# The first two modulation vectors as products on TensorE, and a group of small vectors moved to ScalarE's queue

## The chip, the cores and the metric

The kernel runs on one core of one Trainium2 chip. The metric is the device time of one execution in microseconds (us); lower is better.

## The reference

Two transformer blocks run one after the other over a sequence of 1024 tokens with 1024 channels, all in 32-bit floats. Block one is a gated short-convolution layer and a stick-breaking attention layer; block two has sliding-window and differential attention and a convolutional feed-forward layer. Each layer's input is normalised and modulated, and this is what the change touches:

```python
def modulation(c, w, b, n):
    m = jax.nn.silu(c) @ w + b          # c: 1 x 1024, w: 1024 x 3072
    return jnp.split(m, n, axis=-1)

def modulated_norm(x, g, shift, scale):
    return rmsnorm(x, g) * (1.0 + scale[:, None, :]) + shift[:, None, :]

shift, scale, gate = modulation(c, mod_w, mod_b, 3)   # first layer
h = modulated_norm(x, norm_g, shift, scale)
proj = h @ w_in
```

There are fourteen modulation vectors of 1024 numbers in all, each a product of a vector of 1024 with a matrix of 1024 x 1024. The first two, shift and scale of the first layer, are needed before the first large product `h @ w_in` can begin.

## The kernel before, in words

The activations stand transposed: `X[:, j, t]` holds channel `128*j + partition` of token `t`, in KC = 8 tiles of 128 channels and two halves of 512 tokens. Every large product splits both operands in two parts (`w_hi`, `w_lo` and `opA` or `opB` with parts 0 and 1) and takes three matmuls for each tile; these units, L1255, and pairs of units, L1287, are nearly all the work of TensorE. The program is written out by hand, engine by engine, with semaphores; each engine runs its instructions in the order of its block, and a wait holds back all that stands behind it.

The change lies in the opening, before the first pair of units. There the order is this.

- SyncE's queue loads the small vectors of group 0 into `vec_rows` (L970), rows 0 and 1 of the first modulation matrix into `first_mods[0]` (L978), the eight blocks of `x` into `x_rows` (L984), the rest of the first matrix, the ten small transfers of group 1 and 2 (L970, L990, L992), the first weights, and then the second matrix, `first_mods[1]`. Each matrix comes in eight pieces (`kc`) of 512 KB.
- TensorE transposes group 0 (L1322), then `x` in 16 groups of four (L1333). `norm_sum` (L1303) adds up the squares over the channels; `mod_sum` (L1315) adds a vector that lies spread over 128 partitions.
- ScalarE takes the silu of `c` (L1543), copies each transposed group into `X` (L1550) and squares it (L1529).
- VectorE adds the squares (`sq_add`, L1779) and accumulates the modulation vectors: `first_steps` multiplies each piece of the matrix by its 128 numbers of `c`, one for each partition, and adds them to `mod_acc` (L1860 and L1865). After the eighth piece, `mod_sum` on TensorE adds over the partitions with eight matmuls, each with 128 columns of `mod_acc` as the stationary operand and one column of ones as the moving one. `mod_out` (L1757) adds the bias.
- `parts("a", ...)` on VectorE (L1828, L1836) and `act_parts` on ScalarE (L1507, L1511) then make the operand `opA` tile by tile, and the first pair of units on TensorE (L1287) waits for each tile of it.

The later twelve modulation vectors are accumulated on VectorE between other work, and aren't changed.

Of the kernel before, what the change touches and what calls it, by code (L numbers as in the profile page):

```python
# [12 lines left out]
ALU = mybir.AluOpType  # L13
# [174 lines left out]
def program(nc, a, out, known):  # L188
# [3 lines left out]
    with ctx:  # L192
# [107 lines left out]
        def now(s):  # L300

            return total.get(id(s), 0)
# [660 lines left out]
        def _(sp):  # L963
# [23 lines left out]
            sp.wait_ge(dve_done, at("vec_zero"))  # L987
            vectors(1, ROWS1)
            vectors(2, ROWS2)
            sp.dma_start(small[:, SINK:SINK + 8], a["swa_sinks_2"].to_broadcast([P, 8])).then_inc(vec_in[1], 16)  # L990
            step(vec_in[1], "vec_in", 1, by=16)
            sp.dma_start(lam_rows[:, 0:256], a["diff_lambda_2"].rearrange("o f d -> o (f d)").to_broadcast([P, 256])).then_inc(vec_in[1], 16)  # L992
            step(vec_in[1], "vec_in", 1, by=16)
# [254 lines left out]
        def _(pe):  # L1248
# [57 lines left out]
            def mod_sum(g):  # L1306

                if g < FIRST_MODS:
                    pe.wait_ge(dve_done, at("first_step", g, KC - 1))
                else:  # L1310
                    pe.wait_ge(dve_done, at("mod_step", (g + 1) * MOD_PIECES - 1))
                if g:
                    pe.wait_ge(dve_done, at("mod_out", g - 1))
                for j in range(KC):
                    ins = pe.matmul(PS[:, 6, j:j + 1], mod_acc[:, j * P:(j + 1) * P], ones[:, 0:1], start=True, stop=True)  # L1315
                ins.then_inc(pe_done, 1)
                step(pe_done, "mod_sum", g)


            pe.wait_ge(pool_done, at("consts"))  # L1320
# [3 lines left out]

            for j in range(KC):
# [11 lines left out]
            norm_sum("a", 0)  # L1337
            norm_sum("a", 1)
            mod_sum(0)

# [6 lines left out]
            mod_sum(1)  # L1347
# [76 lines left out]
        def _(act):  # L1424
# [115 lines left out]

            act.wait_ge(dve_done, at("cols"))
# [180 lines left out]
        def _(dve):  # L1722
# [29 lines left out]
            def mod_out(g):  # L1752
# [4 lines left out]
                dve.tensor_tensor(mod[:, g, :], PS[:, 6, 0:KC], cols[:, b:b + KC], ALU.add).then_inc(dve_done, 1)  # L1757
# [91 lines left out]
            def first_steps(g, ks):  # L1849

                for kc in ks:
                    src = SILU_C + 8 * MODS[g][2] + kc
                    c = small[:, src:src + 1]
                    if kc == 0:
                        dve.wait_ge(first_mod_in[g][kc], at("first_mod_in", g, kc))
                        dve.wait_ge(act_done, at("silu_c"))
                        if g:
                            dve.wait_ge(pe_done, at("mod_sum", g - 1))
                        dve.wait_ge(dve_done, now(dve_done))
                        dve.tensor_scalar(mod_acc[:], first_mods[g][:, kc, :], c, None, ALU.mult).then_inc(dve_done, 1)  # L1860
                        step(dve_done, "first_step", g, kc)
                    else:
                        dve.wait_ge(first_mod_in[g][kc], at("first_mod_in", g, kc))
                        dve.wait_ge(dve_done, now(dve_done))
                        dve.scalar_tensor_tensor(out=mod_acc[:], in0=first_mods[g][:, kc, :], scalar=c,  # L1865
                                                 in1=mod_acc[:], op0=ALU.mult, op1=ALU.add).then_inc(dve_done, 1)
                        step(dve_done, "first_step", g, kc)

            first_steps(0, range(2))
            for j in range(KC):  # L1870
                sq_add("a", j, 0)
                sq_add("a", j, 1)
                if j >= 2:
                    first_steps(0, range(j, j + 1))
            mod_out(0)
# [3 lines left out]
            step(dve_done)  # L1879

# [9 lines left out]
            first_steps(1, range(KC))  # L1890
# [252 lines left out]
```

## Time and profile before

| what | before |
|---|---|
| time, median of 3 runs | 3103.62 us (3098.84 to 3111.96) |
| span of the profiled execution | 3091.5 us |
| TensorE matmul busy in it | 2909.7 us, 94% |
| VectorE busy | 1508.1 us, 49% |
| ScalarE busy | 945.4 us, 31% |
| mean granted clock of TensorE | 0.968 |

The span runs from the first to the last instruction; the median lies 12.1 us above it. The views give no time of the profiled execution but its span. A time in a row counts from the span's start. PE is TensorE, PEld its loads of stationary operands, DVE VectorE, ACT ScalarE, POOL GpSimd; SPq and ACTq are the queues in which SyncE and ScalarE issue transfers. A 32-bit float matmul leaves two records, so that the eight matmuls of `mod_sum` show as x16; a transpose leaves one.

### The profile page before, as it was taken

To read this page: it belongs to the slowest core of one execution; us is meant where nothing else is said; L and a number is where in the kernel's file an instruction comes from. 1 tells how busy PE (TensorE), PEld (TensorE's weight loads), DVE (VectorE), ACT (ScalarE), POOL (GpSimd) and SP (SyncE) were. 2 spreads that over 40 slices of the span, in tenths; PEclk is the share of its full clock that TensorE was granted. 3 is DMA by queue.
4 is the path that set the end of the run, shared out by engine and by line. 5 is a ranking of instruction groups with operands and counts; after the bars stand their busy time and mean duration, and the time that the engine had idled before them with its cause. 6 is when DMAs were issued, how large, how long until landed. Compare 5 with 4: busy or idle time off the path is not lost.

```text
span 3091.5 us, 35185 instructions
## 1 busy us (share of the span) xinstructions
PE 2909.7 (94%) x13227; PEld 2331.4 (75%) x13227; DVE 1508.1 (49%) x2270; ACT 945.4 (31%) x1871; POOL 943.4 (31%) x703
## 2 busy tenths in 40 slices
PE   3899999799999999999899999898998999999997
PEld 3688878587786666667688888777886888888886
DVE  5666566632205888874520006775526431451444
ACT  4200001413216787852401007653114110110112
POOL 1233323132234444433233344111332333333321
PEclk7999999899999999999999999898999999999999
DMA  5344444363523333331245125112111111111111
GB/s 194 102 141 144 138 130 143 116 204 123 182 84 96 82 82 82 82 96 48 89 143 191 52 58 164 42 42 82 48 48 41 48 48 48 48 48 48 48 47 70
DMA packets 271510, 287.80 MB, mean 93 GB/s; under 512 B 15043, under 2 KB 216172, under 8 KB 269420
## 3 DMA queue, kind: packets, MB, share of 16 engines
q1 hardware_dynamic: 261580, 241.50, 26.0%
q10 hardware_dynamic: 9760, 44.04, 3.6%
q8 instruction: 105, 1.72, 0.2%
q14 instruction: 65, 0.53, 0.1%
HBM read 228.88 MB, written 56.62 MB: 92 GB/s over the span
## 4 chain that ended last, share of the span: by engine, by line
PE 82%; DVE 9%; ACT 4%; DMA 2%; issue 2%; SPq 0%; POOL 0%; DVEq 0%; ACTq 0%; POOLq 0%
PE PS L1255 63%; PE PS L463 3%; PE PS L1287 3%; PE PS L468 2%; PE PS L600 2%; DVE s_sp L808 1%; DMA mod_raw<-in_w_ada 1%; DVE M L1740 1%; PE PS L569 1%; PE PS L560 1%; PE PS L590 1%; DVE M L1779 1%; PE PS L482 1%; PE PS L1315 1%; DVE s_al L820 1%
## 5 line engine op out<-in xcount | busy, mean ns | idle before, releaser
L1255 PE MATMUL PS<-opA,w_hi 128*128 128x512 f32 x4736 | 1475.7, 392 | 27.3 <-POOL w_lo L1128 11.8
L1255 PEld LDWEIGHTS PS<-opA,w_hi 128*128 128x128 f32 x4736 | 894.7, 189 | 217.2 <-issue 17.1
L1255 PE MATMUL PS<-opA,w_lo 128*128 128x512 f32 x2368 | 925.6, 391 | 0.0
L1123 POOL CAST w_hi<-w_raw 128x1024 fp32r<-128x1024 f32 (+1 forms) x193 | 204.1, 1057 | 1447.9 <-PE PS L1255 1384.6
L1128 POOL TENSOR_TENSOR w_lo<-w_raw,w_hi 128x1024 fp32r<-128x1024 f32 (+1 forms) x198 | 479.3, 2421 | 200.3 <-ACT w_hi L1517 184.8
L1255 PEld LDWEIGHTS PS<-opA,w_lo 128*128 128x128 f32 x2368 | 448.0, 189 | 92.7
L1255 PE MATMUL PS<-opB,w_hi 128*128 128x512 f32 x1216 | 377.9, 391 | 4.4 <-DVE opB L1964 3.4
L1255 PEld LDWEIGHTS PS<-opB,w_hi 128*128 128x128 f32 x1216 | 229.0, 188 | 53.3 <-DVE opB L1964 3.8
L1740 DVE SCALAR_TENSOR_TENSOR M<-mod_raw,small,M 128x512 f32<-128x512 f32 x168 | 186.3, 1109 | 147.7 <-DMA mod_raw<-in_w_ada 70.2
L1255 PE MATMUL PS<-opB,w_lo 128*128 128x512 f32 x608 | 237.2, 390 | 0.0
L1975 DVE SCALAR_TENSOR_TENSOR X<-PS,mod,X 128x512 f32<-128x512 f32 x96 | 72.1, 751 | 290.8 <-PE PS L1255 285.1
L463 PE MATMUL PS<-s_sp,tri 128*128 128x512 f32 (+3 forms) x384 | 167.0, 517 | 19.4 <-DVE s_sp L808 15.5
L808 DVE SCALAR_TENSOR_TENSOR s_sp<-PS,s_t 128x128 f32<-128x128 f32 (+1 forms) x192 | 106.1, 552 | 136.2 <-ACT s_t L678 109.1
L1173 POOL TENSOR_TENSOR s_p<-s_p,s_sp 128x512 f32<-128x512 f32 (+3 forms) x128 | 145.5, 1137 | 63.1 <-DVE s_sp L808 63.1
L820 DVE TENSOR_TENSOR s_al<-s_a,s_ah 128x128 fp32r<-128x128 f32 (+1 forms) x192 | 154.1, 802 | 6.6
L1921 DVE TENSOR_SCALAR yt<-M,cols 128x512 f32<-128x512 f32 x44 | 63.9, 1453 | 164.8 <-ACT M L1687 161.8
L1287 PE MATMUL PS<-opA,w_hi 128*128 128x512 f32 x320 | 118.0, 437 | 21.7 <-DVE opA L1836 21.7
L1687 ACT ACTIVATE M<-PS 128x512 f32<-128x512 f32 x44 | 26.4, 599 | 353.5 <-PE PS L1255 350.9
L1529 ACT ACTIVATE M<-X 128x512 f32<-128x512 f32 x80 | 50.6, 633 | 272.0 <-DVE X L1975 270.7
L1255 PEld LDWEIGHTS PS<-opB,w_lo 128*128 128x128 f32 x608 | 114.6, 188 | 23.8
L468 PE MATMUL PS<-s_p,nones 128*128 128x512 f32 (+3 forms) x320 | 122.5, 465 | 0.0
L653 ACT ACTIVATE s_t<-PS 128x128 f32<-128x128 f32 (+1 forms) x192 | 94.6, 493 | 76.7 <-PE PS L454 42.7
(179 smaller groups left out, 3420.7 us busy)
## 6 DMA issues: line engine op xcount, KB each, us to landing
mod_raw<-in_w_ada SPq DMA_DIRECT2D x96, 256.0 KB, 2.9
w_raw<-in_w_up SPq DMA_DIRECT2D x44, 512.0 KB, 3.8
w_raw<-in_w_in SPq DMA_DIRECT2D x34, 512.0 KB, 3.8
w_raw<-in_a_w_in SPq DMA_DIRECT2D x32, 512.0 KB, 4.8
q_dram<-stage ACTq DMA_DIRECT2D x16, 1024.0 KB, 4.0
hin<-q_dram SPq DMA_DIRECT2D x64, 256.0 KB, 5.5
k_dram<-stage ACTq DMA_DIRECT2D x13, 1024.0 KB, 4.8
mod_raw<-in_b_mod_w SPq DMA_DIRECT2D x48, 256.0 KB, 2.8
```

The source lines that it names most:

```text
L463: ins = pe.matmul(scores_of(g, qs), tri[:], s_sp[:, g % 3, qs:], start=False, stop=True, skip_group_check=True)
L468: ins = pe.matmul(scores_of(g, qp), nones[:], s_p[:, (g - 1) % 3, qp:], start=False, stop=True, skip_group_check=True)
L653: act.activation(s_t[:, g % 3, qs:], scores_of(g, qs), ACT.Abs).then_inc(act_done, 1)
L808: dve.scalar_tensor_tensor(out=s_sp[:, e % 3, qs:], in0=scores_of(e, qs), scalar=0.0, in1=s_t[:, e % 3, qs:], op0=ALU.max, op1=ALU.add).th ...
L820: dve.tensor_tensor(s_al[:, e % 3, qs:], s_a[:, e % 3, qs:], s_ah[:, e % 3, qs:].bitcast(F32), ALU.subtract).then_inc(dve_done, 1)
L1123: pool.tensor_copy(hi, raw).then_inc(pool_done, 1)
L1128: pool.tensor_tensor(lo, raw, hi.bitcast(F32), ALU.subtract).then_inc(pool_done, 1)
L1173: pool.tensor_tensor(s_p[:, g % 3, q0:], s_p[:, (g - 1) % 3, q0:], s_sp[:, g % 3, q0:], ALU.add).then_inc(pool_done, 1)
L1255: ins = pe.matmul(ps, w[:, k0 + k, :], rhs(part, k0 + k), start=(k == 0 and n == 0), stop=(k == chunks - 1 and n == 2))
L1287: ins = pe.matmul(PS[:, 2 * s + hf, :], w[:, s, k, :], op_in[:, part, k, hf * HALF:(hf + 1) * HALF], start=(k == 0 and n == 0), stop=(k == ...
L1740: dve.scalar_tensor_tensor(out=acc, in0=mod_raw[:, n % 2, :], scalar=c, in1=acc, op0=ALU.mult, op1=ALU.add).then_inc(dve_done, 1)
L1975: dve.scalar_tensor_tensor(out=X[:, j, t], in0=PS[:, 2 * (u % 2) + hf, :], scalar=mod[:, gate, j:j + 1], in1=X[:, j, t], op0=ALU.mult, op1 ...
```

## The change

VectorE no longer accumulates the first two modulation vectors. `first_mod(g, kc)` on TensorE takes the piece `kc` of matrix `g` itself as the stationary operand, 128 columns at a time, and the 128 numbers of silu(c) as a moving operand of one column; eight such matmuls for each piece add into eight columns of a PSUM bank, and after the eighth piece the vector is done. Two pieces stand ahead of the transposes of `x` on TensorE, and fourteen behind. `norm_sum` moves behind the fourth piece of the second matrix, since the vectors now use banks 5 and 6 and the second norm sum bank 5. The ten small transfers of groups 1 and 2 are issued by ScalarE, ahead of the silu.

```diff
--- before.py
+++ after.py
@@ -984,13 +984,6 @@
                 sp.dma_start(x_rows[:, tb, :], a["x"][0, tb * P:(tb + 1) * P, :]).then_inc(x_in[tb], 16)
                 step(x_in[tb], "x_in", tb, by=16)
             first_mod(0, range(2, KC))
-            sp.wait_ge(dve_done, at("vec_zero"))
-            vectors(1, ROWS1)
-            vectors(2, ROWS2)
-            sp.dma_start(small[:, SINK:SINK + 8], a["swa_sinks_2"].to_broadcast([P, 8])).then_inc(vec_in[1], 16)
-            step(vec_in[1], "vec_in", 1, by=16)
-            sp.dma_start(lam_rows[:, 0:256], a["diff_lambda_2"].rearrange("o f d -> o (f d)").to_broadcast([P, 256])).then_inc(vec_in[1], 16)
-            step(vec_in[1], "vec_in", 1, by=16)
 
             def mod_loads(pieces):
                 for n in pieces:
@@ -1305,23 +1298,33 @@
 
             def mod_sum(g):
 
-                if g < FIRST_MODS:
-                    pe.wait_ge(dve_done, at("first_step", g, KC - 1))
-                else:
-                    pe.wait_ge(dve_done, at("mod_step", (g + 1) * MOD_PIECES - 1))
-                if g:
-                    pe.wait_ge(dve_done, at("mod_out", g - 1))
+                pe.wait_ge(dve_done, at("mod_step", (g + 1) * MOD_PIECES - 1))
+                pe.wait_ge(dve_done, at("mod_out", g - 1))
                 for j in range(KC):
                     ins = pe.matmul(PS[:, 6, j:j + 1], mod_acc[:, j * P:(j + 1) * P], ones[:, 0:1], start=True, stop=True)
                 ins.then_inc(pe_done, 1)
                 step(pe_done, "mod_sum", g)
 
 
+            def first_mod(g, kc):
+
+                pe.wait_ge(first_mod_in[g][kc], at("first_mod_in", g, kc))
+                pe.wait_ge(act_done, at("silu_c"))
+                for j in range(KC):
+                    ins = pe.matmul(PS[:, 5 + g, j:j + 1], first_mods[g][:, kc, j * P:(j + 1) * P],
+                                    small[:, SILU_C + kc:SILU_C + kc + 1], start=(kc == 0 and j == 0),
+                                    stop=(kc == KC - 1), skip_group_check=True)
+                if kc == KC - 1:
+                    ins.then_inc(pe_done, 1)
+                    step(pe_done, "mod_sum", g)
+
             pe.wait_ge(pool_done, at("consts"))
             pe.wait_ge(vec_in[0], at("vec_in", 0))
             pe.transpose(PS[:, 7, 0:P], vec_rows[:, 0, :], ident[:]).then_inc(pe_done, 1)
             step(pe_done, "vec_T")
 
+            first_mod(0, 0)
+            first_mod(0, 1)
             for j in range(KC):
                 for hf in range(2):
                     n = 2 * j + hf
@@ -1334,17 +1337,21 @@
                                            x_rows[:, 4 * hf + b, j * P:(j + 1) * P], ident[:])
                     ins.then_inc(pe_done, 1)
                     step(pe_done, "x_T", n)
-            norm_sum("a", 0)
-            norm_sum("a", 1)
-            mod_sum(0)
-
+            for kc in range(2, KC):
+                first_mod(0, kc)
             pe.wait_ge(vec_in[1], at("vec_in", 1))
             pe.wait_ge(dve_done, at("cols"))
             for t in (1, 2):
                 ins = pe.transpose(PS[:, 7, t * P:(t + 1) * P], vec_rows[:, t, :], ident[:])
             ins.then_inc(pe_done, 1)
             step(pe_done, "vec_T2")
-            mod_sum(1)
+            for kc in range(KC // 2):
+                first_mod(1, kc)
+            norm_sum("a", 0)
+            pe.wait_ge(dve_done, at("mod_out", 0))
+            norm_sum("a", 1)
+            for kc in range(KC // 2, KC):
+                first_mod(1, kc)
             pe.wait_ge(act_done, at("x_set", 15))
             for j in range(KC):
                 if j == 0:
@@ -1538,6 +1545,20 @@
                     step(act_done, "sq", "n1", j, hf)
 
 
+            act.wait_ge(dve_done, at("vec_zero"))
+            for t, rs in ((1, ROWS1), (2, ROWS2)):
+                r = 0
+                for n, many in rs:
+                    v = a[n]
+                    dims = " ".join(f"d{i}" for i in range(len(v.shape)))
+                    v = v.rearrange(f"{dims} -> ({dims})").rearrange("(r p) -> r p", p=P)
+                    act.dma_start(vec_rows[r:r + many, t, :], v).then_inc(vec_in[1], 16)
+                    step(vec_in[1], "vec_in", 1, by=16)
+                    r += many
+            act.dma_start(small[:, SINK:SINK + 8], a["swa_sinks_2"].to_broadcast([P, 8])).then_inc(vec_in[1], 16)
+            step(vec_in[1], "vec_in", 1, by=16)
+            act.dma_start(lam_rows[:, 0:256], a["diff_lambda_2"].rearrange("o f d -> o (f d)").to_broadcast([P, 256])).then_inc(vec_in[1], 16)
+            step(vec_in[1], "vec_in", 1, by=16)
             act.wait_ge(dve_done, at("cols"))
             act.wait_ge(act_done, now(act_done))
             act.activation(small[:, SILU_C:SILU_C + 16], cols[:, 0:16], ACT.Silu).then_inc(act_done, 1)
@@ -1754,7 +1775,7 @@
                 b = C[MOD_BIAS[name]] + part * KC
                 dve.wait_ge(pe_done, at("mod_sum", g))
                 dve.wait_ge(dve_done, now(dve_done))
-                dve.tensor_tensor(mod[:, g, :], PS[:, 6, 0:KC], cols[:, b:b + KC], ALU.add).then_inc(dve_done, 1)
+                dve.tensor_tensor(mod[:, g, :], PS[:, 5 if g == 0 else 6, 0:KC], cols[:, b:b + KC], ALU.add).then_inc(dve_done, 1)
                 step(dve_done, "mod_out", g)
 
             def gains(gname, scale):
@@ -1846,37 +1867,14 @@
             dve.tensor_copy(cols[:, 0:P], PS[:, 7, 0:P]).then_inc(dve_done, 1)
             step(dve_done, "cols")
 
-            def first_steps(g, ks):
-
-                for kc in ks:
-                    src = SILU_C + 8 * MODS[g][2] + kc
-                    c = small[:, src:src + 1]
-                    if kc == 0:
-                        dve.wait_ge(first_mod_in[g][kc], at("first_mod_in", g, kc))
-                        dve.wait_ge(act_done, at("silu_c"))
-                        if g:
-                            dve.wait_ge(pe_done, at("mod_sum", g - 1))
-                        dve.wait_ge(dve_done, now(dve_done))
-                        dve.tensor_scalar(mod_acc[:], first_mods[g][:, kc, :], c, None, ALU.mult).then_inc(dve_done, 1)
-                        step(dve_done, "first_step", g, kc)
-                    else:
-                        dve.wait_ge(first_mod_in[g][kc], at("first_mod_in", g, kc))
-                        dve.wait_ge(dve_done, now(dve_done))
-                        dve.scalar_tensor_tensor(out=mod_acc[:], in0=first_mods[g][:, kc, :], scalar=c,
-                                                 in1=mod_acc[:], op0=ALU.mult, op1=ALU.add).then_inc(dve_done, 1)
-                        step(dve_done, "first_step", g, kc)
-
-            first_steps(0, range(2))
             for j in range(KC):
                 sq_add("a", j, 0)
                 sq_add("a", j, 1)
-                if j >= 2:
-                    first_steps(0, range(j, j + 1))
-            mod_out(0)
             dve.wait_ge(pe_done, at("vec_T2"))
             dve.wait_ge(dve_done, now(dve_done))
             dve.tensor_copy(cols[:, P:3 * P], PS[:, 7, P:3 * P]).then_inc(dve_done, 1)
             step(dve_done)
+            mod_out(0)
 
             for i in range(2):
                 dve.wait_ge(vec_in[1], at("vec_in", 1))
@@ -1887,7 +1885,6 @@
             dve.wait_ge(dve_done, now(dve_done))
             dve.reduce_sum(small[:, LAM:LAM + 2], lam_rows[:, 512:640].rearrange("p (i d) -> p i d", i=2), AX_X).then_inc(dve_done, 1)
             step(dve_done, "lam_sum")
-            first_steps(1, range(KC))
             mod_out(1)
             parts("a", "a_norm_g", A_SCALE, None)
 
```

On TensorE, the order between the last transposes of `x` (L1333) and the first pair of units (L1287) was this, in the kernel before. `M_56` holds the sums of squares and `M_58` is `mod_acc`; the moving operand stands ahead of the comma, the stationary one behind it.

```order
L1333 MATMUL PS<-ident,x_rows 128x128 x3
L1303 MATMUL PS<-M_56,ones 128x512 [waits pool_done,dve_done] x2
L1315 MATMUL PS<-ones,M_58 128x1 [waits dve_done]
L1315 MATMUL PS<-ones,M_58 128x1 x7
L1344 MATMUL PS<-ident,vec_rows 128x128 [waits dve_done,vec_in1]
L1344 MATMUL PS<-ident,vec_rows 128x128
L1315 MATMUL PS<-ones,M_58 128x1 [waits dve_done]
L1315 MATMUL PS<-ones,M_58 128x1 x7
L1287 MATMUL PS<-opA,w_hi 128x512 [waits pool_done,dve_done,act_done]
```

It held sixteen matmuls of one column (L1315). After the change the same place reads as follows; `first_mod_68` and `first_mod_69` are the two matrices, L1336 is the transpose of `x` and L1314 the new matmul. The pieces left out repeat the pattern.

```order
L1336 MATMUL PS<-ident,x_rows 128x128 x3
L1314 MATMUL PS<-small,first_mod_68 128x1 [waits act_done,first_mod_in0_2]
L1314 MATMUL PS<-small,first_mod_68 128x1 x7
...
L1345 MATMUL PS<-ident,vec_rows 128x128 [waits dve_done,vec_in1]
L1345 MATMUL PS<-ident,vec_rows 128x128
L1314 MATMUL PS<-small,first_mod_69 128x1 [waits act_done,first_mod_in1_0]
L1314 MATMUL PS<-small,first_mod_69 128x1 x7
...
L1296 MATMUL PS<-M_56,ones 128x512 [waits pool_done,dve_done] x2
L1314 MATMUL PS<-small,first_mod_69 128x1 [waits act_done,first_mod_in1_4]
...
L1314 MATMUL PS<-small,first_mod_69 128x1 [waits act_done,first_mod_in1_7]
L1314 MATMUL PS<-small,first_mod_69 128x1 x7
L1280 MATMUL PS<-opA,w_hi 128x512 [waits pool_done,dve_done,act_done]
```

Fourteen pieces of eight one-column matmuls now stand between the transposes of `x` and the first pair, with the two norm sums (L1296) ahead of the last four of them.

On ScalarE, the opening after the change is this; before it, the first row was the table load.

```order
L1555 DMA vec_rows<-in_b_ada 48x128 [waits dve_done]
L1555 DMA vec_rows<-in_final_norm_g 8x128
L1555 DMA vec_rows<-in_norm_g 8x128 x2
L1555 DMA vec_rows<-in_final_g 8x128
L1555 DMA vec_rows<-in_conv_b 22x128
L1555 DMA vec_rows<-in_diff_subln_g 1x128
L1555 DMA vec_rows<-in_conv_w 66x128
L1558 DMA small<-in_swa_sinks 128x8
L1560 DMA lam_rows<-in_diff_lambda 128x256
L1564 ACT_TABLE_LOAD [waits act_done]
L1564 ACTIVATE small<-cols 128x16 [waits dve_done]
L1571 ACTIVATE X<-PS 128x512 [waits act_done,pe_done]
```

The ten transfers now stand ahead of the silu (L1564) and the first copy of `x` (L1571).

## Rows read from the trace of the kernel before

**Rows 1.** The page: busy time by engine, then the chain that ended last.

```profile
PE 2909.7 (94%) x13227; PEld 2331.4 (75%) x13227; DVE 1508.1 (49%) x2270; ACT 945.4 (31%) x1871; POOL 943.4 (31%) x703
...
PE 82%; DVE 9%; ACT 4%; DMA 2%; issue 2%; SPq 0%; POOL 0%; DVEq 0%; ACTq 0%; POOLq 0%
```

**Rows 2.** The chain that ended last, 0 to 160 us: start us, us, what.

```profile
8.55 10.74 DMA x_rows<-in_x
...
61.08 1.30 DVE M L1865
62.42 3.58 PE PS L1315 x16
66.03 0.18 DVE mod L1757
...
69.57 25.93 PE PS L1287 x93
```

**Rows 3.** TensorE in order of time: start us, us, line, shapes, count [idle before].

```profile
14.31 1.09 PE L1333 MATMUL PS<-ident,x_rows 128*128 128x128 f32 x4 [8.48 <-DMA x_rows<-in_x]
19.43 5.37 PE L1333 MATMUL PS<-ident,x_rows 128*128 128x128 f32 x28 [4.03 <-DMA x_rows<-in_x]
25.26 0.66 PE L1333 MATMUL PS<-ident,x_rows 128*128 128x128 f32 x4 [0.46 <-ACT X L1550]
...
35.14 1.12 PE L1333 MATMUL PS<-ident,x_rows 128*128 128x128 f32 x4 [0.30 <-ACT X L1550]
44.77 3.41 PE L1303 MATMUL PS<-M,ones 128*128 128x512 f32 x4 [8.51 <-DVE M L1779]
48.02 1.84 PE L1315 MATMUL PS<-ones,M 128*128 128x1 f32 x16
49.72 0.42 PE L1344 MATMUL PS<-ident,vec_rows 128*128 128x128 f32 x2
62.42 3.57 PE L1315 MATMUL PS<-ones,M 128*128 128x1 f32 x16 [12.28 <-DVE M L1865]
```

**Rows 4.** VectorE and ScalarE in order of time, same columns.

```profile
0.91 0.27 DVE L1842 MEMSET vec_rows<- 128x256 f32 x1 [0.91 <-PEq L2137]
...
7.79 0.75 DVE L1860 TENSOR_SCALAR M<-first_mod,small 128x1024 f32<-128x1024 f32 x1 [1.63 <-DMA first_mod<-in_a_mod_w]
52.75 9.61 DVE L1865 SCALAR_TENSOR_TENSOR M<-first_mod,small,M 128x1024 f32<-128x1024 f32 x7
...
0.85 1.28 ACT L1543 ACT_TABLE_LOAD   x1 [0.85 <-PEq L2137]
6.19 0.22 ACT L1543 ACTIVATE small<-cols 128x16 f32<-128x16 f32 x1 [4.06 <-DVE cols L1846]
...
40.82 0.63 ACT L1529 ACTIVATE M<-X 128x512 f32<-128x512 f32 x1
```

**Rows 5.** TensorE's matmul records at L1315 in the whole kernel: duration ns min/median/max.

```profile
L1315 PE MATMUL PS<-ones,M x224: 164/250/370, 48.0 to 674.5; 128*128 128x1 f32 x112
```

**Rows 6.** Stretches of TensorE: us, PE busy (records), PEclk, DMA share, GB/s.

```profile
27.00:29.00 2.00, 0.98 (x8) 1.00 0.28 89
...
30.00:31.00 1.00, 0.25 (x3) 0.80 0.96 303
...
47.00:48.00 1.00, 1.00 (x2) 0.66 0.01 4
48.00:49.00 1.00, 1.00 (x11) 1.00 0.00 0
...
50.00:52.00 2.00, 0.14 (x2) 0.77 0.03 8
...
74.00:75.00 1.00, 1.00 (x4) 0.51 0.00 0
```

**Rows 7.** Transfer issues on the queues of SyncE and ScalarE.

```profile
13.26 1.08 SPq L970 DMA_DIRECT2D vec_rows<-in_b_ada  x1
...
L1609 ACTq DMA_DIRECT2D q_dram<-stage x16: 366/366/460, 792.2 to 1582.1; - x16
```

## The prediction

> **What bounds the kernel now.** The page comes first: TensorE is busy for 94% of the span and carries 82% of the chain that ended last [rows 1]. So a microsecond counts where TensorE waits, and the change lies in the opening, the one long place where it does. I then followed the chain there [rows 2]. The load of `x` ends at 19.3 us; from then the chain goes through transposes, squares and the accumulation on VectorE, until the last step of the second vector at 61.08 us, `mod_sum(1)` at 62.42, `mod_out(1)` at 66.03, and at 69.57 the first pair of units. The number that decides is thus the start of `mod_out(1)`: 66.0 us. The 3.5 us from there to the pair (gain, first tile of `opA`) aren't touched, and behind the pair everything hangs on the instruction before it, so a shift of this start goes into the end one for one.
>
> TensorE in that stretch [rows 3] stands idle for 8.5 us ahead of the norm sums and 12.3 us ahead of `mod_sum(1)`. VectorE works: the last seven steps take 9.61 us [rows 4]. That is part of the work that the change removes. The question is what it costs on TensorE.
>
> **What the change removes.** Sixteen accumulation steps on VectorE and sixteen one-column matmuls on TensorE. VectorE is then free early: ScalarE's last square ends at 41.45 us [rows 4], and the squares are summed a microsecond or so later. Nothing else on VectorE stands in the way.
>
> **What it adds on TensorE.** 16 pieces of 8 matmuls are 128 matmuls, 16 of them ahead of the transposes of `x`. The shape is that of `mod_sum`, 128 x 128 stationary and one column moving, so the trace has the price at both levels of the clock. At 62.42 us, 16 records took 3.57 us [rows 3], the longest record is 0.37 us [rows 5]; with that as the one that ends the row, (3.57 - 0.37) / 15 is 0.213 us from record to record, 0.427 us a matmul, 3.41 us a piece. The granted clock is at its lower level of 1.2 GHz here. At 48.02 us the same 16 records took 1.84 us, with the clock at 2.4 GHz [rows 3, 6]; less the median record of 0.25 us [rows 5] that is 0.106 us a record, 0.212 us a matmul, 1.70 us a piece. The cost is loading: each matmul loads 128 columns twice to stream one.
>
> On this price the Trainium skill, "TensorE: Matmul & The Clock Gate", section "LDWEIGHTS (loading the stationary operand)", gives columns divided by 1.2, in ns. That is 107 ns for a load of 128 columns, and by my estimate 112 x 2 x 107 ns = 23.9 us for the matmuls behind the transposes. Row and page agree in the fast row alone; in the slow row the measured distance is double, and the measurement decides.
>
> **The pieces ahead of `x`.** The first piece has landed at 7.8 us, when VectorE takes it [rows 4]. Two pieces at the low clock take 6.8 us and end at 14.6. The transposes of the first half of `x` began at 14.31; the second half comes at 19.43 [rows 3], so half a microsecond lost there is covered by the wait for the data. Cost: nothing; if that cover were gone, up to 6.8 us.
>
> **The pieces behind `x`.** The last group of transposes starts at 35.14 and ends at 36.26 us [rows 3]. Groups follow at ScalarE's pace (a copy and a square each), not TensorE's, so this end stays. All of the matrices have landed by 47 us, where the transfers stop [rows 6]; TensorE reaches the second matrix later than that. From 36.26 us to the end of the last piece TensorE has nothing to wait for; it is one queue of work: 14 pieces (112 matmuls), the transposes of the second group of vectors (0.42 us) and the four records of the norm sums, 3.41 us at the low clock [rows 3]. At the low clock that is 112 x 0.427 = 47.8, plus 0.4, plus 3.4, 51.6 us, and about 0.15 us for the last record to end: 88.0 us. Against 66.0 this is **22.0 us later**. At the full clock it would be 23.7 + 0.3 + 1.7 = 25.7 us, done at 62.1: 3.9 us earlier. The clock decides the sign.
>
> **Which clock.** The page shows 1.00 from the start, but the first group of four transposes took 1.09 us, as at 35.14 (1.12), and not 0.66 as at 25.26 [rows 3]: TensorE began at the lower level and rose in the unbroken run of 28 transposes at 19.43. It fell again at about 30.5, after groups that kept it busy for half of the time [rows 6]. So it is low at 36 us. The question is whether a stream of one-column matmuls raises it. Two rows speak to that. In the norm sums, which stream 512 columns a record, the clock rose 2.9 us after they began. Then came `mod_sum(0)`, 1.84 us of one-column matmuls without a gap, and two transposes, and by the row of 50 to 52 us the clock fell again at about 51.1 [rows 6]: in the last 3 us TensorE had been occupied for 2.1, and nearly all of it by the one-column stream and loads. At 27 to 29 us transposes that kept it busy for 0.98 of 2 us had still been granted the full clock, and for 1.6 us more. The one-column stream counted for no more than they did, though it was denser. The other row, 3.57 us of it at 62.42, stayed at the low clock to its end, where the norm sums had brought a rise in 2.9. I take it that this stream does not raise the clock.
>
> The norm sums inside the stream may raise it for a while, as they did before; the full clock then lasted from 47.7 us (0.66 of full speed over 47:48) to 51.1 (0.77 over 50:52), about 3.4 us [rows 6]. Time at the full clock does twice the work, so it would save 3.4 us. Against it, the first pair, begun at 69.57, got the full clock only at 75 [rows 2, 6]; so both are equally near, and I take half, -1.7 us. Bounds: 0 and -3.4.
>
> **The ten transfers.** SyncE needed 1.08 us for the first of them; ScalarE's issues of large transfers take 0.37 us [rows 7]. Ten are 3.7 us, or 5.1 if two of them take 1.08, from 1.2 us on, when the memset that they wait for ends; with the table load of 1.28 us behind them the silu starts at 6.2 to 7.6, before at 6.19 [rows 4]. With its 0.22 us it ends at 7.8 at the latest, when the first piece lands. On the transfer side they leave SyncE's queue, where the DMA share had dropped to 0.28 [rows 6], so the second matrix comes some 2 to 3 us earlier: worth nothing, as it isn't waited for. In return they now share the engines with `x`. They are 0.22 MB (169 rows of 512 bytes, 128 of 32 and 128 of 1024), which at the 303 GB/s of 30:31 is 0.7 us; bounds 0 and 2 us, the length of the thin stretch at 27:29 [rows 6]; I take 0.3 us, because a part passes before the loads of `x` start.
>
> **Sum.** 22.0 - 1.7 + 0.3 = 20.6 us. On the span of 3091.5 us that is 3112.1; the median of the runs lies 12.1 us above the span, so I forecast **3124 us**, 0.66% slower. A measurement of this kernel can tell about 0.5%, 15.5 us, from no change.
>
> **The rivals.** (a) *The one-column stream raises the clock*, and the change ends not slower. Say the clock rises c us after 36.26: the queue takes 25.7 + c / 2, and it breaks even with the 29.7 us that there were at c = 8 us. With the 5 us that the first pair needed (69.57 to 75) [rows 2, 6], `mod_out(1)` starts at 64.6: 1.4 us gained, 3102 us. For it speaks that TensorE is without a gap for 50 us, far longer than any of the rows; against it, the fall at 51.1. The Trainium skill, "TensorE: Matmul & The Clock Gate", section "Why this matters for your kernels", asks only that TensorE be kept busy continuously to reach the full clock; by that rule this rival is the forecast. Chance 0.17. (b) *The clock swings within the stream*, since pieces, transposes and norm sums mix, or the norm sums raise it twice: full for 10 to 40 us of the 52, 3106 to 3119 us, chance 0.08. (c) *The ten transfers hold back `x`*: each us that its last block lands later moves the transposes, the squares and the queue behind them by one; with 5 us it is 3129 us. Against it: 0.2 MB among 13. Chance 0.05, on the slow side. (d) *The earlier matrix pays*: it would have to be what VectorE or TensorE waits for, but the transfers are done at 47 and VectorE's last seven steps on it began at 52.75 [rows 4, 6]. Worth 0. The forecast's own case has 0.70.
>
> **How the numbers follow.** In the forecast's case the time is 3120 to 3131: 18.6 us to 24 us on the median, with 2.5 us on either side for the phase in which the clock rises in the first pair. That case and (c) hold 0.75. To leave out less than 2 in 10, the range goes down through (b) and into (a): 3100 to 3131. Slower by over 0.5%: (c) and most of the own case, as 20.6 stands 5 us above the bound while the medians of this kernel move by several us, 0.67. Faster by over 0.5% needs 15 us that nothing offers: 0.02. The rest, 0.31, is within 0.5%.
>
> **What would show it.** Between the last transpose of `x` and the first pair the profile after should have TensorE busy without a gap, 224 records at L1314 at 0.213 us distance and PEclk 0.50 in nearly all stretches, and the pair's start at 88 to 93 us. VectorE should idle there instead, waiting for L1314. The prediction is wrong if PEclk goes to 1.00 within some 8 us of the last transpose and stays, if the one-column matmul with its stationary operand fresh from a transfer has another price than 0.21 or 0.43 us, or if the pair's start moves and the end does not follow.

## The result, and the profile after

| what | before | after |
|---|---|---|
| time, median of 4 runs | 3107.79 us (3098.84 to 3121.15) | 3136.68 us (3132.16 to 3148.73) |
| ratio, 95% interval | | 1.0093 (1.0057 to 1.0128) |
| span of the profiled execution | 3091.5 us | 3130.4 us |
| first pair of units starts | 69.57 us | 95.11 us |
| mean granted clock of TensorE | 0.968 | 0.958 |

The change makes the kernel slower by 0.9%: 28.9 us on the medians, where 20.6 were forecast. The sign was right, and so was the mechanism of the largest term; the price of the ten transfers was not. The time lies 5.7 us above the range. The profiled execution's own time was 3132.16 us, 1.8 us above its span. The 12.1 us between median and span of the kernel before are thus mostly scatter: the execution that was profiled there was a short one.

TensorE in order of time, the kernel after, in the columns of [rows 3]:

```profile
8.29 7.11 PE L1314 MATMUL PS<-small,first_mod 128*128 128x1 f32 x32 [2.26 <-DMA first_mod<-in_a_mod_w]
18.27 1.09 PE L1336 MATMUL PS<-ident,x_rows 128*128 128x128 f32 x4 [2.86 <-DMA x_rows<-in_x]
23.39 6.54 PE L1336 MATMUL PS<-ident,x_rows 128*128 128x128 f32 x32 [4.04 <-DMA x_rows<-in_x]
...
39.09 1.12 PE L1336 MATMUL PS<-ident,x_rows 128*128 128x128 f32 x4 [0.29 <-ACT X L1571]
40.00 20.48 PE L1314 MATMUL PS<-small,first_mod 128*128 128x1 f32 x96
60.34 0.67 PE L1345 MATMUL PS<-ident,vec_rows 128*128 128x128 f32 x2
60.80 13.65 PE L1314 MATMUL PS<-small,first_mod 128*128 128x1 f32 x64
74.32 3.76 PE L1296 MATMUL PS<-M,ones 128*128 128x512 f32 x4
77.87 13.65 PE L1314 MATMUL PS<-small,first_mod 128*128 128x1 f32 x64
95.11 0.77 PE L1280 MATMUL PS<-opA,w_hi 128*128 128x512 f32 x1 [3.58 <-DVE opA L1857]
```

From 40 us to the end of the last piece TensorE is never idle. 96 one-column records in 20.48 us are 0.213 us a record, the price forecast from [rows 3, 5]. The granted clock in that stretch (the figure behind the count of records; the last two are the transfer engines' share and GB/s):

```profile
36.00:48.00 12.00, 11.14 (x51) 0.50 0.92 308
48.00:60.00 12.00, 12.00 (x58) 0.50 0.01 2
60.00:72.00 12.00, 12.00 (x59) 0.50 0.00 0
72.00:84.00 12.00, 12.00 (x46) 0.50 0.00 0
84.00:95.00 11.00, 7.52 (x36) 0.50 0.01 1
```

TensorE was busy for 50 us without a gap and stayed at 1.2 GHz all the way, through the norm sums at 74.32 too. The two longest waits for TensorE in the opening (who waited, on what: us in total, times, longest) show who stood idle meanwhile:

```profile
ACT M L1448 <- PE PS L1296: 29.7, 1, 29.7
DVE mod L1778 <- PE PS L1314: 28.8, 1, 28.8
```

What was not forecast stands at the top of the first fence: the transposes of `x` begin at 18.27 and 23.39 us, where they began at 14.31 and 19.43 in [rows 3]. `x` comes 4.0 us late, and 0.3 had been allowed for that.

### The profile page after: what moved, and what is told of

It is laid out like the page before. It is cut to its first block, busy times and chain, and to the rows that moved or that the text cites. A ratio compares the mean times of both kernels' runs of the same rounds, so it can differ in the third digit from the quotient of the medians.

```text
span 3130.4 us, 35615 instructions
## 1 busy us (share of the span) xinstructions
PE 2978.8 (95%) x13451; PEld 2398.4 (77%) x13451; DVE 1488.1 (48%) x2254; ACT 945.2 (30%) x1871; POOL 941.5 (30%) x703
## 4 chain that ended last, share of the span: by engine, by line
PE 81%; DVE 9%; ACT 5%; issue 2%; DMA 2%; SPq 0%; POOL 0%; DVEq 0%; ACTq 0%; POOLq 0%
PE PS L1248 62%; PE PS L1280 3%; PE PS L463 2%; PE PS L468 2%; PE PS L600 2%; PE PS L1314 2%; PE PS L569 1%; DVE s_sp L808 1%; PE PS L544 1%; DVE s_al L820 1%; DMA mod_raw<-in_w_ada 1%; DVE M L1761 1%; ACT s_t L653 1%; PE PS L560 1%; PE PS L590 1%
## 5 line engine op out<-in xcount | busy, mean ns | idle before, releaser
L1248 PE MATMUL PS<-opA,w_hi 128*128 128x512 f32 x4736 | 1475.6, 392 | 27.9 <-POOL w_lo L1121 11.8
```

The lines of the kernel that those rows point to most:

```text
L1248: ins = pe.matmul(ps, w[:, k0 + k, :], rhs(part, k0 + k), start=(k == 0 and n == 0), stop=(k == chunks - 1 and n == 2))
```

## Where the time went, stretch by stretch

The two traces hold the same matmuls from the first pair on. The difference between the start times of the same instruction in both goes like this (worked out from the traces, not a view):

| at, in the kernel before | later in the kernel after |
|---|---|
| 69.57 us, first pair | 25.5 us |
| 140 to 1960 us | 25.2, rising to 26.5 us |
| 2400 us to the end | 40.1 us |

So the opening's 25.5 us go through the kernel one for one, as forecast. The other 13.5 us of this pair of profiles arise between 1960 and 2400 us of the kernel before, mostly in the second block's attention, which the change doesn't touch. The experiments below take both parts apart.

## The experiments

In the kernels below the part named is all that differs, with the PSUM banks and waits that it needs; all compute the whole reference. Ratios are against the kernel before on the same chip.

**The products alone.** The change with the ten transfers put back on SyncE:

```diff
             first_mod(0, range(2, KC))
+            sp.wait_ge(dve_done, at("vec_zero"))
+            vectors(1, ROWS1)
+            vectors(2, ROWS2)
+            sp.dma_start(small[:, SINK:SINK + 8], ...)
+            sp.dma_start(lam_rows[:, 0:256], ...)
...
-            act.dma_start(vec_rows[r:r + many, t, :], v).then_inc(vec_in[1], 16)
-            act.dma_start(small[:, SINK:SINK + 8], ...)
-            act.dma_start(lam_rows[:, 0:256], ...)
```

> The change with its ten transfers put back on SyncE's queue at their old place, so that only the products on TensorE are left of it. Theory: the change's 25.5 us at the first pair of units (95.11 us against 69.57) are 21.5 us of one-column matmuls at the low clock and 4.0 us by which the ten transfers hold back x. Then x's second half reaches the transposes at 19.4 us and the pair starts at 91.1 us, PEclk 0.50 all through the one-column stream. Rival: the two pieces that TensorE takes ahead of x, or their loads, are what delays x; then the pair stays at 95.1 us. Total: 21.5 us over the kernel before, give or take the scatter of the runs of some 10 us.

Measured: ratio 1.0067 (1.0036 to 1.0097). TensorE in order of time:

```profile
14.84 1.09 PE L1343 MATMUL PS<-ident,x_rows 128*128 128x128 f32 x4
19.61 4.12 PE L1343 MATMUL PS<-ident,x_rows 128*128 128x128 f32 x24 [3.68 <-DMA x_rows<-in_x]
...
70.55 3.42 PE L1303 MATMUL PS<-M,ones 128*128 128x512 f32 x4
...
88.20 0.76 PE L1287 MATMUL PS<-opA,w_hi 128*128 128x512 f32 x1 [3.58 <-DVE opA L1850]
```

and its granted clock around the norm sums:

```profile
70.00:80.00 10.00, 10.00 (x52) 0.67 0.01 2
```

`x`'s second half is in time to 0.2 us, so the two pieces ahead of it don't delay it; the transfers do. The pair starts at 88.20 us, 18.6 us later than before, and not at 91.1 with the low clock all through, as expected: here the clock did rise beside the norm sums (0.67 over 70 to 80 us is 3.4 us of full clock), and the one-column records in that time went twice as fast. From the start of the norm sums to the pair it is 17.65 us, in the changed kernel's profile 20.79. So 3.1 us were saved, close to the bound of -3.4 us that the prediction gave; the changed kernel's profile shows the other bound, 0.

**The transfers alone.** The mirror image, the kernel before with `act.dma_start` for the ten.

> The kernel before with nothing changed but the ten small transfers, issued by ScalarE ahead of the silu. Theory: they slow the loads of x by themselves; the transposes of x's second half start at 23.4 us in place of 19.43, and as VectorE's chain hangs on them, the first pair starts at 73.5 us (4.0 later). Rival: it takes the reads of TensorE as well; then x is in time, 19.4 and 69.6 us. A second rival: VectorE absorbs the delay, since it waits for squares between its steps; then x is 4 us late and the pair under 2 us.

Measured: ratio 1.0007 (0.9983 to 1.0032). TensorE in order of time:

```profile
22.43 4.12 PE L1326 MATMUL PS<-ident,x_rows 128*128 128x128 f32 x24 [4.03 <-DMA x_rows<-in_x]
...
50.48 3.78 PE L1296 MATMUL PS<-M,ones 128*128 128x512 f32 x4 [11.22 <-DVE M L1786]
54.06 3.41 PE L1308 MATMUL PS<-ones,M 128*128 128x1 f32 x16
```

`x` is 3.0 us late, so the transfers do it by themselves. The pair was later by more: it started at 77.43 us, 7.9 us late. The norm sums begin 5.7 us later than in [rows 3], and `mod_sum(0)` behind them ran at the low clock, in 3.41 us where it took 1.84, with VectorE's second accumulation waiting for it. VectorE's sums of squares lost more than `x` did because single instructions among them ran long: two of its additions took 2.66 and 2.64 us here (at 34.01 and 45.60 us), where most take 0.69. Long ones stand in the kernel before too, 3.1 us over the usual in all against 5.3 here (worked out from the traces). Why they run long stays open. The ratio can't tell the 7.9 us from nothing.

**The matrix as the moving operand.** The same products on TensorE, roles exchanged; transfers on SyncE:

```diff
-                for j in range(KC):
-                    ins = pe.matmul(PS[:, 5 + g, j:j + 1], first_mods[g][:, kc, j * P:(j + 1) * P],
-                                    small[:, SILU_C + kc:SILU_C + kc + 1], start=(kc == 0 and j == 0),
-                                    stop=(kc == KC - 1), skip_group_check=True)
+                for h in range(2):
+                    ins = pe.matmul(PS[0:1, ROW_BANKS[g][h], :], small[:, SILU_C + kc:SILU_C + kc + 1],
+                                    first_mods[g][:, kc, h * HALF:(h + 1) * HALF], start=(kc == 0), stop=(kc == KC - 1))
...
+                for j in range(KC):
+                    ins = pe.matmul(PS[:, 2 + g, j:j + 1], mod_rows[0:1, g, j * P:(j + 1) * P],
+                                    ones[0:1, 0:1], start=True, stop=True)
```

> The products as in the run with the products alone, but with the operands in exchanged roles: the 128 numbers of silu(c) are the stationary operand (one column), the piece of the matrix moves through in two matmuls of 512 columns; the row of 1024 that comes out is copied by VectorE and brought back into columns by eight small matmuls. Same numbers of multiplications. Theory: the clock stayed low because one-column matmuls do not count as activity; with 512 columns moving it rises within some 5 us of the last transposes of x, a piece takes 1.7 us at the full clock, and the pair starts at about 73 to 75 us. Rival: something else of this stage holds the clock low (32-bit operands, the loads that still land); a piece then takes 3.4 us and the pair starts at 98 us or later.

Measured: ratio 0.9995 (0.9961 to 1.0030). TensorE in order of time, then its granted clock:

```profile
36.08 12.49 PE L1323 MATMUL PS<-first_mod,small 128*1 128x512 f32 x24
48.49 0.44 PE L1362 MATMUL PS<-ident,vec_rows 128*128 128x128 f32 x2
48.87 7.03 PE L1323 MATMUL PS<-first_mod,small 128*1 128x512 f32 x16
...
73.53 0.77 PE L1289 MATMUL PS<-opA,w_hi 128*128 128x512 f32 x1 [3.58 <-DVE opA L1863]
```

```profile
36.00:40.00 4.00, 4.00 (x6) 0.50 1.02 418
40.00:44.00 4.00, 4.00 (x10) 0.98 1.11 342
44.00:56.00 12.00, 12.00 (x30) 1.00 0.22 69
```

The clock rose some 4 us into the wide stream and stayed to its end. Four pieces take 7.03 us, 1.8 us a piece, and the pair starts at 73.5 us, as expected. So nothing else in this stage holds the clock low; the shape does. Whether it is the one moving column or the 128 stationary columns loaded anew for each matmul, this run doesn't separate. It isn't that a piece costs fewer cycles as a row: a piece is four records of 512 columns, and the four of the norm sums took 3.55 us at 1.2 GHz to the start of the next row (74.32 to 77.87 in the first fence), no less than the 3.41 us of a piece in one-column matmuls. With the products as rows the pair is 4.0 us later than before in place of 18.6, although turning the rows back into columns comes on top. At least 14.7 of the 18.6 us were thus the clock.

**Which of the transfers.** Four variants of the changed kernel: only the eight transfers of vector rows with ScalarE; only the two broadcasts; all ten with the broadcasts first; all ten behind `act.wait_ge(x_in[3], at("x_in", 3))` and the silu.

> The changed kernel with only the two broadcast transfers (the sinks, 128 rows of 32 bytes, and the lambdas, 128 rows of 1024 bytes) put back on SyncE's queue at their old place; the eight transfers of vector rows stay with ScalarE. Theory: the broadcasts, whose packets run beside the loads of x between 6 and 12 us, are what thins these loads; then the transposes of x's second half start at 19.4 to 20 us. Rival: ScalarE's issues beside SyncE's slow x, or the rows of 512 bytes; then it stays at 22 to 23.4 us.

> The counterpart: the eight transfers of vector rows are back on SyncE's queue, the two broadcasts stay with ScalarE ahead of the silu. Theory (the broadcasts thin the loads of x): the transposes of x's second half start at 22 to 23.4 us. Rival: at 19.4 to 20 us.

> The changed kernel with the ten transfers on ScalarE in another order: the two broadcasts first, then the eight of vector rows, all still ahead of the silu. Neither the broadcasts alone nor the rows alone on ScalarE had delayed x (19.78 and 19.60 us). Theory: in the changed kernel the broadcasts stand at the end of ScalarE's queue and their packets run beside the loads of x from 6 us on; issued first they are through before, and the transposes of x's second half start at 19.5 to 20 us. Rival: what counts is that ScalarE still issues when SyncE begins to issue x at 5.0 us, whichever transfer it is; then they start at 22 to 23.4 us.

> The changed kernel with the ten transfers still on ScalarE and in their order, but behind the silu and a wait for the fourth block of x, so at about 14 us, when SyncE has issued all of x. If packets of the broadcasts beside loads of x are what costs, the second half of x, which is on its way then, comes up to 2 us late (20 to 21.5 us). If it is the overlap of the two engines' issues, x is in time at 19.4 to 19.8 us, and in its place the loads of the first matrix behind it are thinned. ScalarE's ten issues end at about 18 us, before the second half of x in either case.

| ScalarE issues | SyncE's eight issues of `x` | transposes of `x`'s second half | first pair |
|---|---|---|---|
| none (the kernel before; again) | 4.02 us; 4.05 us | 19.43 us; 19.52 us | 69.57 us; 69.84 us |
| all ten, broadcasts last, without the products | 6.05 us | 22.43 us | 77.43 us |
| all ten, broadcasts last (the change; again) | 6.36 us; 6.33 us | 23.39 us; 22.39 us | 95.11 us; 91.00 us |
| eight vector rows only | 4.03 us | 19.60 us | 88.19 us |
| two broadcasts only | 4.15 us | 19.78 us | 88.38 us |
| all ten, broadcasts first | 4.25 us | 20.33 us | 88.93 us |
| all ten, from 14.3 us | 4.08 us | 19.67 us | 91.40 us |

The last four have one execution each, so their times say nothing; their openings do. (In the last one the norm sums left the clock low, which accounts for the 91.40.) My first theory was too simple: the broadcasts on ScalarE cost at most 0.3 us when they are alone and 0.9 us when they come first (the second of these runs went against its expectation, the third lies 0.3 us above its own). What costs 3 to 4 us is the two broadcasts at the end of ScalarE's ten. That the two engines issue at the same time isn't it: with the broadcasts first ScalarE issues to 5.26 us, longer than in the changed kernel (5.10), and `x` is nearly in time. The transfer engines' share and GB/s (last two figures) in the kernel before, in the changed kernel, with broadcasts last, and in the variant with broadcasts first:

```profile
6.00:8.00 2.00, 1.00 0.97 397
8.00:10.00 2.00, 1.00 1.03 410
```

```profile
6.00:8.00 2.00, 1.00 0.67 225
8.00:10.00 2.00, 1.00 0.67 230
10.00:12.00 2.00, 1.00 0.68 249
12.00:14.00 2.00, 1.00 1.03 379
```

```profile
6.00:8.00 2.00, 1.00 0.98 350
8.00:10.00 2.00, 1.00 1.04 415
```

For six microseconds the engines move 225 to 249 GB/s in place of some 410, with a third of their time idle, while the broadcasts' packets pass among those of `x`. With the transfers from 14.3 us, the thin stretch moved to 22 to 26 us (277 and 294 GB/s) and fell on the first matrix instead. The expectation had named that outcome as the sign of overlapping issues, but the run can't decide it: the broadcasts' packets passed from 21.1 us on, when `x` had landed. On SyncE's queue the stretch stands at 26 to 30 us, in the kernel before:

```profile
26.00:28.00 2.00, 1.00 0.37 108
28.00:30.00 2.00, 1.00 0.54 164
```

With the two broadcasts alone on SyncE it is there too, and with the eight vector rows alone it is gone (26 to 28 us in both):

```profile
26.00:28.00 2.00, 1.00 0.28 82
```

```profile
26.00:28.00 2.00, 1.00 1.15 287
```

It goes with the broadcasts in every one of these profiles in which they pass beside or between large loads, and is absent when they pass before these. The packets in the changed kernel's trace tell the two apart: up to 8.8 us only those of 32 bytes pass, from 9.0 to 11.8 only those of 1024, and the rate is low in both, 225 at 6 to 8 us and 249 at 10 to 12. By what mechanism wasn't tried.

**The kernel before once more.** Nothing edited.

> The kernel before once more, for its profile and for the scatter of its runs. Theory: the 13 us by which the profile of the changed kernel lies above the 25.5 us of the opening come from the stage of the second attention, 1976 to 2170 us, where the clock is granted low for 65 us in one execution and 109 in another by chance; then this profile, of the same kernel, has its first pair at 69.5 to 70 us and yet a span that differs from 3091.5 us by 5 to 30 us, with 0.3 to 0.45 us for each us more at the low clock in that stage. Rival: the stage reacts to the shift of what comes ahead of it; then this span is within 3 us of 3091.5.

Measured: ratio 0.9998 (0.9971 to 1.0026). Its first pair started at 69.84 us and its span was 3102.8 us, 11.3 us longer than the other profile of the same kernel. The stage with the second attention, between the same two matmuls, in the kernel before, in this run, in the kernel after, in its second profile and in the products alone (us, busy, clock):

```profile
1960.00:2400.00 440.00, 404.96 (x2052) 0.92 0.16 51
```

```profile
1961.00:2411.00 450.00, 419.52 (x2050) 0.89 0.16 50
```

```profile
1987.00:2440.00 453.00, 423.81 (x2050) 0.88 0.16 49
```

```profile
1981.00:2423.00 442.00, 409.01 (x2051) 0.91 0.16 51
```

```profile
1989.00:2454.00 465.00, 436.08 (x2055) 0.85 0.15 48
```

The same work takes 440 to 465 us as the clock is granted, 440 and 450 in one and the same kernel, and 453 and 442 in the changed one. Over all 14 profiles of this study its length follows the time at the low clock in it: 411.8 us and 0.378 us for each us at 1.2 GHz (correlation 0.996; 55 to 154 us of it, 433 to 471 us long; worked out from the traces). So the stage's scatter is enough for the 13.5 us. That the change adds nothing to it is shown by the next comparison, to within some 8 us.

**The changed kernel once more.**

> The changed kernel once more, for its profile and for more runs of it. Expected from the opening alone: 25.5 us over the kernel before when the norm sums don't raise the clock, 22 when they do, so a ratio of 1.007 to 1.009; first pair at 92 to 95.2 us. The stage of the second attention puts 5 to 30 us of scatter on it, with 0.35 us for each us at the low clock there.

Measured: ratio 1.0085 (1.0057 to 1.0112). The pair started at 91.0 us, with `x` 3.0 us late and a rise of the clock beside the norm sums; the span was 3113.5 us, as the attention stage took 442 us this time. The mean span of its eleven runs is 22.1 us above that of the kernel before beside them, and the opening is 21.2 to 25.5 us longer: nothing is left over for the stages behind it.

**Two versions that share the work.** VectorE keeps the first vector. In one, TensorE takes four pieces of the second matrix as one-column products in its idle time and adds VectorE's part to them; in the other it makes the whole second vector as a row. The core of the second:

```diff
+            for kc in range(4):
+                row_piece(kc)
             norm_sum("a", 0)
             norm_sum("a", 1)
             mod_sum(0)
...
-            mod_sum(1)
+            for kc in range(4, KC):
+                row_piece(kc)
+            row_cols()
...
-            first_steps(1, range(KC))
+            dve.wait_ge(pe_done, at("mod_row"))
+            for h in range(2):
+                dve.tensor_copy(mod_row[0:1, h * HALF:(h + 1) * HALF], PS[0:1, ROW_BANKS[h], :]).then_inc(dve_done, 1)
```

> The kernel before with one part of the idea: VectorE accumulates the first vector and pieces 4 to 7 of the second as before, TensorE takes pieces 0 to 3 of the second matrix as one-column products while it would stand idle (two ahead of the norm sums, two behind mod_sum(0)) and adds VectorE's part into the same eight columns. Theory: TensorE's idleness before mod_sum(1) was 8.5 and 12.3 us, so 13.7 us at the low clock lie beside VectorE's work, which is four steps of 1.39 us shorter: the pair starts at 64 to 65 us (5 us earlier), the whole some 5 us faster, less than a measurement tells. Rival: the pieces delay the norm sums and mod_sum(0), on which VectorE's second accumulation waits; then the gain is 0 to 2 us.

> The kernel before with the first vector accumulated on VectorE and the second made on TensorE alone, with the matrix as the moving operand (512 columns a matmul), four pieces ahead of the norm sums and four behind mod_sum(0); the row is copied by VectorE and brought into columns by eight small matmuls. The ten transfers stay on SyncE. Theory: the wide stream raises the clock, so that a piece takes 1.7 us and mod_sum(0) 1.8; the row is done at about 56 us and the pair starts at 62 to 64 us, 6 to 7 us earlier than the 69.57 before, and over many runs the kernel is 0.2% faster. Rival: the clock is low where the stream begins and the four pieces hold back the norm sums and mod_sum(0); then the gain is 3 us or less.

> The version with the second vector as a row on TensorE once more, for a tighter interval. Its opening was 6.7 us shorter. Expected: ratio 0.996 to 0.9985 if it is the opening alone; the first pair at 63 to 64 us.

| version | first pair starts | ratio, 95% interval |
|---|---|---|
| four one-column pieces shared | 66.58 us | 0.9971 (0.9940 to 1.0002) |
| second vector as a row | 63.19 us | 0.9962 (0.9932 to 0.9992) |
| the same again | 65.73 us | 0.9930 (0.9903 to 0.9956) |

The row version is faster than both kernels. Its opening is 3.8 to 6.4 us shorter, which is 0.12 to 0.21%; the second comparison shows more, at least 13 us by its interval (0.9956 of 3111 us), which the opening doesn't explain and which lies outside its expectation. The pair, too, came later than the 63 to 64 us expected, as the clock fell for 3.4 us at 49.7. The two medians of the row version agree (3093.1 and 3092.3 us); those of the kernel before beside them were 3109.0 and 3111.3. Most of the rest lies in the clock behind the opening. As the granted clock is either 0.5 or 1, time at the low clock is 2 x (1 - clock) x span; by the means of the second comparison it is 188 us a run against 251, of which 23 us fall in the opening. Over 80 runs of the kernel before, the span grows by 0.373 us for each such us (correlation 0.97), so the other 40 are worth some 15 us. The means of the runs differ by 22.7 us, and the opening leaves 18.7 of them. Why the clock was granted for longer there stays open. The one-column version gained 3.0 us at the pair, not 5: `mod_sum(0)` fell into the low clock there (3.41 us) and held back VectorE's second half.

## Why the prediction was right in kind and off in size

- *The price of the one-column stream*: 0.213 us a record at the low clock was forecast and measured (20.48 us for 96). Two small prices were read from rows at another clock: 0.42 us for two transposes (0.67 at 1.2 GHz) and 3.41 us for the norm sums (3.76); the queue as a whole came out 0.4 us shorter than forecast all the same.
- *The clock*: the step on which the sign hung. The reading of the fall at 51.1 us [rows 6] held: 50 us of the stream did not raise the clock, and the wide stream did so in 4 us. Rival (a) is out. The pair was forecast for 88 to 93 us and came at 95.11 and, in the second profile, 91.00. The section "Why this matters for your kernels" of "TensorE: Matmul & The Clock Gate" in the Trainium skill would have TensorE kept busy continuously to reach the full clock; the trace disagrees for this stream, which kept TensorE busy for 51 us at 0.50, and the measurement decides.
- *The norm sums*: between 0 and -3.4 us, taken at -1.7. Both ends occur, and nothing between: of the seven profiles with all products in one-column matmuls, two saved nothing (20.8 us from the norm sums to the pair, the changed kernel's first profile among them) and five saved 3.1 us (17.7 us). Which of the two comes was not forecast and isn't explained here.
- *One for one to the end*: held, as the table of stretches shows.
- *The ten transfers*: this term of the sum was mis-sized. It stood at 0.3 us, bounds 0 and 2, from their bytes; it measured 3.0 and 4.0 us. The step that failed is to price small transfers by their bytes. [rows 6] had shown at 27 to 29 us that they leave the engines thinly used, at 89 GB/s, where they pass. The prediction took the length of that one row as its upper bound, and less than the bytes' time as its value. The stretch was longer: by the rows of 26 to 30 us shown above the engines moved there, against 410 GB/s, what amounts to 2.7 us too little (an estimate: (302 + 246) x 2 / 410). Rival (c) named the delay of `x`, at a chance of 0.05, but not its mechanism.
- *The base and the range*: 28.9 us were measured against 20.6. The opening of the profile gives 25.5, that is 21.6 of products (the queue behind `x` ran for 51.35 us, 51.75 were worked out) and 3.9 of transfers: 3.6 more than forecast for the transfers, 1.7 more for the norm sums, 0.4 less for the queue. The other 3.4 lie within the scatter. With these 25.5 us on the first median, 3103.62, the time would have been 3129.1 and inside the range. It lay outside because that median itself moved to 3107.79 with a fourth run, and because the range held no scatter: 80 further runs of the kernel before span 3089.5 to 3131.9 us. Three runs over 13 us in the table were the sign of it.

## What to carry to other kernels

Ask of work moved to TensorE what it streams, not only how long it keeps the engine occupied: here a 32-bit matrix-vector product with the matrix stationary paid for two loads of 128 columns a matmul and left the clock low, while the same product with the matrix moving cost about the same cycles and brought the full clock, for the price of turning a row back into columns. Price small and broadcast transfers by the stretch of the trace in which they pass, and when they change queue, look at what they will then pass beside. Before a difference of 10 us is read into one profile, compare the same stage in two profiles of the same kernel.

## What the runs showed of the hardware that was not expected

- One-column float matmuls with 128 new stationary columns each time, 160 records and two transposes without a gap from 40.00 to 74.3 us: granted clock 0.50 throughout. Matmuls with one stationary column and 512 moving: 1.00 after some 4 us.
- Two broadcast transfers of 4 and 128 KB, issued last of ten small ones from a second queue, took the loads beside them from some 410 to 225 to 249 GB/s for six microseconds (211 to 279 in the second profile), and the issues of `x` on the first queue from 4.0 to 6.4 us. Issued first, they cost 0.9 us at most.
- A stage of small matmuls in dependence on other engines took 433 to 471 us for the same work, by the share of it that was granted the low clock, from execution to execution of the same kernel as well (440 and 450 us).
